# Attention scores of two heads at a time, each on 64 rows of the array, with queries and keys stored without zero halves and the attention units taken in pairs of heads

## What is computed

```python
# first block, heads of 64; memory heads the same against n_mem=256 keys
s = jnp.einsum('bshd,bmhd->bhsm', q, k) * (HEAD_DIM ** -0.5)
# forgetting attention, causal, c = cumsum(log_f)
s = jnp.einsum('bhqd,bhkd->bhqk', qi, k) * scale
s = s + ci[..., :, None] - c[..., None, :]
s = jnp.where(kpos[None, :] <= qpos[:, None], s, -jnp.inf)
p = jax.nn.softmax(s, axis=-1)
o = jnp.einsum('bhqk,bhkd->bhqd', p, v)
# selected and window branch, g: 2 key heads, r: 4 query heads of each
s = jnp.einsum('bgrqd,bgnd->bgrqn', qi, k_branch) * scale
```

## Time and profile before

| | before |
|---|---|
| median of 3 runs | 2407.84 us (2404.71 to 2408.11) |
| profiled execution, its own time | 2406.65 us |
| its span of instructions | 2404.9 us |
| mean granted TensorE clock | 0.989 |
| busy: TensorE, its weight loads | 2345.4 us (98%), 1920.0 us (80%) |
| busy: VectorE, ScalarE, GpSimd | 1201.9, 612.6, 1484.0 us |

### The profile page before, as it was taken

One profiled execution on the slowest core, in us unless ns is written; L12 is line 12 of the kernel. 1 busy time (PEld: TensorE's weight loads), 2 busy tenths in 40 slices (PEclk: granted clock), 3 DMA queues, 4 the chain that ended last, 5 costly groups with the idle time before them and its releaser, 6 DMA issues.

```text
span 2404.9 us, 30922 instructions
## 1 busy us (share of the span) xinstructions
PE 2345.4 (98%) x11620; PEld 1920.0 (80%) x11620; DVE 1201.9 (50%) x1924; ACT 612.6 (25%) x1343; POOL 1484.0 (62%) x677
## 2 busy tenths in 40 slices
PE   6999999999999999999999999999999999999998
PEld 5877788888887878888888888877788888888886
DVE  6567667773353265557642143542555567330422
ACT  4335522221021153332220021111443322210210
POOL 5650377778865613336788888754323358887884
PEclk9999999999999999999999999999999999999999
DMA  5220123333323301112233333332101112233331
GB/s 194 82 77 1 34 89 96 97 97 105 105 88 105 110 22 36 45 53 71 84 101 97 97 97 99 101 98 87 62 27 45 44 62 96 94 99 97 96 97 70
DMA packets 53837, 195.87 MB, mean 81 GB/s; under 512 B 6096, under 2 KB 6096, under 8 KB 53456
## 3 DMA queue, kind: packets, MB, share of 16 engines
q1 hardware_dynamic: 51408, 187.72, 24.2%
q10 hardware_dynamic: 2304, 6.37, 0.7%
HBM read 191.97 MB, written 2.10 MB: 81 GB/s over the span
## 4 chain that ended last, share of the span: by engine, by line
PE 92%; DVE 4%; DMA 1%; issue 1%; ACT 1%; POOL 1%; SPq 0%; DVEq 0%; POOLq 0%; ACTq 0%
PE bank L420 25%; PE bank L422 24%; PE bank L421 24%; PE bank L527 6%; PE bank L558 5%; PE bank L538 3%; PE bank L496 1%; PE bank L436 1%; PE bank L457 1%; PE bank L487 0%; PE bank L531 0%; DMA w_raw<-wstream 0%; DVE vbd L1468 0%; PE bank L667 0%; PE bank L529 0%
## 5 line engine op out<-in xcount | busy, mean ns | idle before, releaser
L370 POOL TENSOR_TENSOR w_hi<-w_raw,zero 128x1024 fp32r<-128x1024 f32 x336 | 643.2, 1914 | 868.1 <-PE bank L422 782.3
L373 POOL TENSOR_TENSOR w_lo<-w_raw,w_hi 128x1024 fp32r<-128x1024 f32 x336 | 842.4, 2507 | 26.3
L420 PE MATMUL bank<-hn_hi,w_hi 128*128 128x512 f32 x1632 | 660.5, 405 | 23.9 <-POOL w_lo L373 11.3
L422 PE MATMUL bank<-hn_hi,w_lo 128*128 128x512 f32 x1632 | 640.0, 392 | 0.0
L421 PE MATMUL bank<-hn_lo,w_hi 128*128 128x512 f32 x1632 | 639.2, 392 | 0.0
L420 PEld LDWEIGHTS bank<-hn_hi,w_hi 128*128 128x128 f32 x1632 | 309.2, 189 | 92.0 <-DVE conv_in L1349 9.8
L422 PEld LDWEIGHTS bank<-hn_hi,w_lo 128*128 128x128 f32 x1632 | 308.2, 189 | 66.7
L421 PEld LDWEIGHTS bank<-hn_lo,w_hi 128*128 128x128 f32 x1632 | 309.2, 189 | 60.5 <-issue 2.2
L420 PE MATMUL bank<-hid_hi,w_hi 128*128 128x512 f32 x688 | 267.6, 389 | 0.0
L421 PE MATMUL bank<-hid_lo,w_hi 128*128 128x512 f32 x688 | 267.6, 389 | 0.0
L422 PE MATMUL bank<-hid_hi,w_lo 128*128 128x512 f32 x688 | 267.6, 389 | 0.0
(11 more groups left out here) (305 smaller groups left out, 3005.8 us busy)
## 6 DMA issues: line engine op xcount, KB each, us to landing
w_raw<-wstream SPq DMA_DIRECT2D x352, 512.0 KB, 3.5
x<-xT SPq DMA_DIRECT2D x4, 512.0 KB, 7.8
out<-yout ACTq DMA_DIRECT2D x8, 256.0 KB, 2.2
mem_x<-memT SPq DMA_DIRECT2D x1, 1024.0 KB, 13.1
lnc<-lncount ACTq DMA_DIRECT2D x1, 1024.0 KB, 6.0
cs<-trig ACTq DMA_DIRECT2D x2, 512.0 KB, 3.5
par<-params ACTq DMA_DIRECT2D x1, 696.0 KB, 8.9
fc<-fconst ACTq DMA_DIRECT2D x1, 592.0 KB, 6.9
```

The source lines that it names most:

```text
L370: nc.gpsimd.tensor_tensor(w_hi[:, slot, :], w_raw[:, slot, :], zeros, ALU.add).then_inc(w_rounded, 1)
L373: nc.gpsimd.tensor_tensor(w_lo[:, slot, :], w_raw[:, slot, :], w_hi[:, slot, :].bitcast(f32), ALU.subtract).then_inc(w_split, 1)
L420: nc.tensor.matmul(ps[bank][:, 0:cols_], wh, a_h, start=c == 0, stop=False)
L422: mm = nc.tensor.matmul(ps[bank][:, 0:cols_], wl, a_h, start=False, stop=c == chunks - 1)
```

## The change

Heads come in pairs. In `U1` and `UF` a pair is heads 2p and 2p+1, in `UN` heads p and p+4 (which share a column of `qb` and use the first and second key head). Within the pair of heads the units run over t, for "fox", "sel" and "win" in the order 0, 2, 1, 3. At even steps TensorE makes the scores of units i and i+1: the first reads only partitions 0 to 63 of queries and keys, the second only 64 to 127, and each writes its own bank. Their mask and gate matmuls come behind both. New waits stand ahead of each score for its bank: for the minimum ("b1") or the exponential (others) of unit u-3. VectorE takes both minima at even steps. The key tiles lose their second, zero half; each is filled by one operation over 128 partitions in place of two over 64, and the memsets are gone. The steps of transposes, value products, fillers and output scaling stay one unit each.

```diff
-        k1 = at("k1", [4, 2, S], f32, R + 8 * KIB)
+        k1 = at("k1", [4, S], f32, R + 8 * KIB)
...
-        km = at("km", [2, 2, NMEM], f32, R + 36 * KIB)
+        km = at("km", [2, NMEM], f32, R + 36 * KIB)
...
-        ka = at("ka", [4, 2, S], f32, R + 8 * KIB)
+        ka = at("ka", [4, S], f32, R + 8 * KIB)
...
-        ksw = at("ksw", [2, 2, S], f32, R + 40 * KIB)
+        ksw = at("ksw", [2, S], f32, R + 40 * KIB)
...
-        U1 = [("b1", h, t) for h in range(8) for t in range(TT)] + [("mem", h, t) for h in range(4) for t in range(TT)]
-        UF = [("fox", h, t) for h in range(8) for t in range(TT)]
-        UN = [(k, h, t) for k in ("sel", "win") for h in range(8) for t in range(TT)]
+        T_ORDER = (0, 2, 1, 3)
+        U1 = ([("b1", 2 * p + r, t) for p in range(4) for t in range(TT) for r in range(2)]
+              + [("mem", 2 * p + r, t) for p in range(2) for t in range(TT) for r in range(2)])
+        UF = [("fox", 2 * p + r, t) for p in range(4) for t in T_ORDER for r in range(2)]
+        UN = [(k, p + 4 * r, t) for k in ("sel", "win") for p in range(4) for t in T_ORDER for r in range(2)]
...
                 for i in range(u0, u1 + 4):
-                    if i < u1:
...
-                        mm = nc.tensor.matmul(bank[:, 0:w], q_, k_, start=True, stop=plain)
-                        if kind == "fox":
-                            nc.tensor.matmul(bank[:, 0:w], headsel[0:96, h, :], c3[0:96, 0:w], start=False, stop=False)
-                        if not plain:
-                            mm = nc.tensor.matmul(bank[:, t * P:w], identb, causal, start=False, stop=True)
-                        mm.then_inc(scored, 1)
+                    if i < u1 and (i - u0) % 2 == 0:
...
+                        for u in (i, i + 1):
+                            _, h, t = units[u][:3]
+                            r = slice(HD * (u - i), HD * (u - i) + HD)
+                            if kind == "b1":
+                                q_, k_ = q1[r, h // 2, t * P:(t + 1) * P], k1[r, h // 2, :]
...
+                            else:
+                                q_ = qb[r, h % 4, t * P:(t + 1) * P]
+                                k_ = ksw[r, 0 if kind == "sel" else 1, 0:w]
+                            if u - u0 < 3 and gates_from is not None:
+                                pe.wait_ge(*took(last_on_bank[u % 3]))
+                            if u - u0 >= 3:
+                                pe.wait_ge(row_min if units[u - 3][0] == "b1" else row_exp, u - 2)
+                            mm = nc.tensor.matmul(ps[u % 3][:, 0:w], q_, k_, start=True, stop=plain)
+                            if plain:
+                                mm.then_inc(scored, 1)
+                        for u in () if plain else (i, i + 1):
+                            _, h, t = units[u][:3]
+                            bank = ps[u % 3]
+                            if kind == "fox":
+                                nc.tensor.matmul(bank[:, 0:w], headsel[0:96, h, :], c3[0:96, 0:w], start=False, stop=False)
+                            nc.tensor.matmul(bank[:, t * P:w], identb, causal, start=False, stop=True).then_inc(scored, 1)
...
                         elif kind == "kz":
-                            A(ka[0:64, idx, 0, :], src[0:64, :], ACT.Copy)
-                            A(ka[64:128, idx, 1, :], src[64:128, :], ACT.Copy).then_inc(act_took, 1)
+                            A(ka[:, idx, :], src[:, :], ACT.Copy).then_inc(act_took, 1)
...
-                    if i < u1:
-                        kind, h, t = units[i][:3]
-                        w, mn = width(i), cols[:, 0, i % 64:i % 64 + 1]
-                        dve.wait_ge(scored, i + 1)
+                    for u in (i, i + 1) if i < u1 and (i - u0) % 2 == 0 else ():
+                        kind, h, t = units[u][:3]
+                        w, mn = width(u), cols[:, 0, u % 64:u % 64 + 1]
+                        dve.wait_ge(scored, u + 1)
...
-            V.memset(km[64:128, :, 0, :], 0.0)
-            V.memset(km[0:64, :, 1, :], 0.0)
...
-                    V.memset(k1[64:128, :, 0, :], 0.0)
-                    link(V.memset(k1[0:64, :, 1, :], 0.0))
...
-                V.memset(ka[64:128, :, 0, :], 0.0)
-                V.memset(ka[0:64, :, 1, :], 0.0)
-                V.memset(ksw[64:128, :, 0, :], 0.0)
-                V.memset(ksw[0:64, :, 1, :], 0.0)
...
-                            V.tensor_tensor(ksw[0:64, idx, 0, :], ps[5][0:64, :], t1[0:64, :], ALU.add)
-                            V.tensor_tensor(ksw[64:128, idx, 1, :], ps[5][64:128, :], t1[64:128, :],
-                                            ALU.add).then_inc(roped, 1)
+                            V.tensor_tensor(ksw[:, idx, :], ps[5][:, :], t1[:, :], ALU.add).then_inc(roped, 1)
```

More of the change, by code:

```diff
@@ L509, in attend @@
                 for i in range(u0, u1 + 4):
-                    if i < u1:
-                        kind, h, t = units[i][:3]
[L512 to L521, removed]
+                    if i < u1 and (i - u0) % 2 == 0:
+                        kind, w = units[i][0], width(i)
                         plain = kind in ("b1", "mem")
@@ L524, in attend @@
                             pe.wait_ge(qk_final, len(QK))
-                        if i - u0 < 3 and gates_from is not None:
-                            pe.wait_ge(*took(last_on_bank[i % 3]))
-                        mm = nc.tensor.matmul(bank[:, 0:w], q_, k_, start=True, stop=plain)
-                        if kind == "fox":
-                            nc.tensor.matmul(bank[:, 0:w], headsel[0:96, h, :], c3[0:96, 0:w], start=False, stop=False)
-                        if not plain:
-                            mm = nc.tensor.matmul(bank[:, t * P:w], identb, causal, start=False, stop=True)
-                        mm.then_inc(scored, 1)
+                        for u in (i, i + 1):
[3 more added lines that the diff above has]
+                                q_, k_ = q1[r, h // 2, t * P:(t + 1) * P], k1[r, h // 2, :]
+                            elif kind == "mem":
+                                q_, k_ = qm[r, h // 2, t * P:(t + 1) * P], km[r, h // 2, :]
+                            elif kind == "fox":
+                                q_, k_ = qa[r, h // 2, t * P:(t + 1) * P], ka[r, h // 2, 0:w]
+                            else:
[14 more added lines that the diff above has]
+                            nc.tensor.matmul(bank[:, t * P:w], identb, causal, start=False, stop=True).then_inc(scored, 1)
                     j = i - 2
@@ L957, in _ @@
                         else:
[L958 to L961, removed]
+                            A(km[:, idx, :], ps[bank][:, 0:w], ACT.Identity, scale=pcol("mk_g")).then_inc(qk_raw, 1)
                         if t not in ROPE:
@@ L1229, in attend @@
                         V.tensor_tensor(sg[:, g, :], ps[3][:, :], rs[:, :], ALU.mult).then_inc(dve_took, 1)
-                    if i < u1:
-                        kind, h, t = units[i][:3]
-                        w, mn = width(i), cols[:, 0, i % 64:i % 64 + 1]
-                        dve.wait_ge(scored, i + 1)
+                    for u in (i, i + 1) if i < u1 and (i - u0) % 2 == 0 else ():
+                        kind, h, t = units[u][:3]
+                        w, mn = width(u), cols[:, 0, u % 64:u % 64 + 1]
+                        dve.wait_ge(scored, u + 1)
                         if kind == "b1":
-                            if i - 2 >= u0:
-                                dve.wait_ge(row_exp, i - 1)
-                            V.tensor_tensor_reduce(out=srow[:, i % 2, :], in0=ps[i % 3][:, :], in1=lnc[:, t, :], scale=1.0,
+                            if u - 2 >= u0:
+                                dve.wait_ge(row_exp, u - 1)
+                            V.tensor_tensor_reduce(out=srow[:, u % 2, :], in0=ps[u % 3][:, :], in1=lnc[:, t, :], scale=1.0,
                                                    scalar=3e38, op0=ALU.add, op1=ALU.min, accum_out=mn).then_inc(row_min, 1)
                         else:
-                            V.tensor_reduce(mn, ps[i % 3][:, 0:w], AX.X, ALU.min).then_inc(row_min, 1)
+                            V.tensor_reduce(mn, ps[u % 3][:, 0:w], AX.X, ALU.min).then_inc(row_min, 1)
                     if u0 == 0:
@@ L1393, in _ @@
                         else:
-                            V.tensor_tensor(k1[0:64, idx, 0, :], ps[7][0:64, :], part[0:64, :], ALU.mult)
-                            V.tensor_tensor(k1[64:128, idx, 1, :], ps[7][64:128, :], part[64:128, :],
-                                            ALU.mult).then_inc(qk_final, 1)
+                            V.tensor_tensor(k1[:, idx, :], ps[7][:, :], part[:, :], ALU.mult).then_inc(qk_final, 1)
                     elif kind == "qm":
@@ L1401, in _ @@
                         dve.wait_ge(qk_raw, e + 1)
-                        V.tensor_tensor(km[0:64, idx, 0, :], ps[7][0:64, 0:w], km[0:64, idx, 0, :], ALU.mult)
```

(3 more changed lines are left out.)

## The result

The changed kernel takes **2361.36 us** (median of 4 runs, 2360.79 to 2364.78) where the kernel before takes 2407.61 (4 runs beside it, 2404.71 to 2408.11): a ratio of 0.9814, 95% interval 0.9803 to 0.9826. Two more jobs with the same kernel gave 2361.85 (0.9815, 0.9799 to 0.9832) and 2363.57 (0.9822, 0.9810 to 0.9835); in the second of them one run of six took 4238.6 us at a granted clock of 0.816 and is left out.

The account below looks back on a forecast made before the run. TensorE, busy 98% of the span and carrying 92% of the chain, was taken as the bound. Overlap -21.2, shape changes +37.6 and zero halves -2.5 made +13.9 us on 2406.65: 2420.6 us, range 2374 to 2434.

Parts of the forecast that it names:

- Part 1: Paired scores: head b's first record starts at best with head a's second, a pair takes 3m; 21.2 us saved.
- 2m per pair: Paired scores, m being one record's time: best-case saving if both heads run wholly side by side, 63.6 us in all.
- The bracket around it: Bounds on the paired scores' saving: at worst nothing, at best both heads wholly together, 63.6 us.
- Width 128: The 24 score pairs of 128 columns: nothing saved, as four weight loads bound them.
- Part 2: Around each score pair the array changes shape twice: emptying of 0.09 to 0.10 us plus bared loads, 37.6 us lost.
- the exit to the mask matmul: Return from paired scores to a bf16 mask matmul, whose load is shorter: estimated at 0.15 us.
- Cheap switches: Rival on the shape changes: half price, 18.8 us, giving 2401.8 or 2391.2 us; chance 0.20.
- Part 3: Order of units and waits in the attention steps: moved loads and new waits are covered, costed at 0.
- The new bank wait: Head b's score waits for the exponential of unit i-2; 2.6 us of TensorE work at width 512 covers it: 0.
- Part 4: Zero halves of key tiles: 1.1 us of km memsets and 1.4 us of ksw evictions go, -2.5 us.
- The clock's part: After the ksw stops, the 2.4 GHz level may be kept: at most half of 6.5 us, twice; taken as 0.
- wholly together: Rival on paired scores: both heads overlap fully, 63.6 us saved, total -28.5, 2378.2 us; chance 0.18.

Follow-up runs that it names:

- e_aabb: Changed kernel with each score matmul issued twice, both of head a ahead of both of head b: 2429.11 us (1.0093).
- e_single: Changed kernel, 64-row scores kept, but one unit scored at each step, so no overlap and twice the visits: 2537.12 us (1.0542).

## Why the prediction was wrong

**Part 1 is the step that failed**: "A2 needs the rows that A1 uses and starts m later; B1 stands behind A2, so it can at best start with A2". This took TensorE to start matmuls in the order of the program whatever rows they use. B1 starts 6 to 7 ns behind A1, past A2, and e_aabb shows it past three waiting records. Saved are 2m per pair, 63.6 us at the widths of 256 and more in place of 21.2. The bracket around it was right, its upper end was the truth, and I chose a value inside it by a rule that no row of before could show, since none has two tiles. The Trainium skill's "TensorE: Matmul & The Clock Gate", Part 3, The mechanism, lets tiles in different rows overlap, but has matmuls start strictly in program order; the order is not borne out between two row tiles by e_aabb (186.047 ahead of 186.996). The Trainium skill's "TensorEngine Tiling (Array Packing)", Key Properties, says that tiles operate independently and load and multiply in parallel, and that is what this trace shows (0.30 us for four loads). I had cited both pages, and took from them the program order and the drain, not the independence.

**Width 128** was costed at 0, "bound by its four loads". The loads pair up as well: 0.22 saved for each of 24 pairs, 5.3 us before the visit is paid.

**Part 2 held.** The price from L767's columns, 0.09 to 0.10 of emptying and then a bare load, was right for rows: 35.0 us by the trace, 37.6 forecast, and e_single measures 0.30 and 0.24 a visit. Only the exit to the mask matmul was 0.04 too dear. "Cheap switches" falls.

**Part 3 costed the order at 0 and missed 11.5 us** (9.1 for the order, 1.5 of it the clock's, and 2.4 for pairs). The wait that the order removes was in the trace of before, L420 at 948.32 with 0.50 us; I looked for covers that the change might break, not for waits that it might cure, and the chain counts such a delay as TensorE's own. The new bank wait, also costed at 0, did cost: 1.3 us in the first block and 1.4 in forgetting attention.

**Part 4 held**: start -1.1, each ksw stop 0.70 shorter (3.49 to 2.79 us by the chains), -2.5 together. The clock's part was within its noise.

**The sum again** with what was measured: -68.8 + 35.0 - 11.5 - 2.5 + 2.7 = -45.1, against -45.9 of span. That this comes so close is partly luck: in attention the sum has 1.2 us more than the stages show (-42.6, measured -41.4), and outside it 2.0 less (-2.5, measured -4.5; the kernel before ran at 1.2 GHz for 3.4 us at 684.7, and the changed one has no such dip there). The rival "wholly together" (-28.5) had the mechanism; 5.3 (width 128), 11.5 (order and pairs) and 2.6 (switches), less 2.7 (new waits), are the 17 us between it and this sum. It got a chance of 0.18 because "my rows are silent", while the forecast, on which they were as silent, got 0.32.

**The signs named beforehand**: B1 beside A1, not 0.1 behind A2 (wrong); the load 0.09 clear of the stream ahead (right); counts the same (right); the first block's 48 units within 1 us (they fell 7.9; and the forecast's own terms for them, 7.2 paid and 6.0 saved, gave 1.2 longer, outside this sign); selected/window longer by 4 to 8 us a layer (it fell 11.9); the km memsets gone from the chain (right).

## What to carry to other kernels

Two fp32 matmuls whose contractions of 64 rows lie in different halves of the array run wholly side by side, loads and all, in either order of issue, as long as neither waits for its bank: count a pair at the time of one. Look there for new waits: one that head b's late turn used to hide is now in the open. Each visit to that shape and back costs 0.24 to 0.31 us here, which is worth it from about 256 columns for one pair (0.43 saved) and for narrower ones only when several share a visit. And when a change reorders work, go through the waits of the kernel before as well: a reordering that costs nothing may be worth as much as the change it came with.

## What was not expected of the hardware

- Each half of the rows keeps its own line of waiting matmuls: starts 6 to 7 ns apart past one waiting record, 13 to 14 ns apart past three. How many it can hold isn't shown.
- With single 64-row scores between whole-array work the granted clock was 0.50 for 147 us from the first block on and 34 us in memory attention, with TensorE 99% busy in the first block; with the scores two by two the first block ran at 1.00. In forgetting and selected/window attention single scores kept 1.00.
